# Shifting the six places of a weight ring by 16 bytes from one to the next

## What is computed

```python
x = x + 0.5 * swiglu(rmsnorm(x, ffn1_norm[l]), w_ffn1_in[l], w_ffn1_out[l])
u = rmsnorm(x, mix_norm[l])
c_q, c_kv, k_r, hq, hf, hi, hgate, mq, gate_logits = split_sizes(u @ w_in[l], IN_SPLITS)
y_mla, y_hg, y_mem = ... # three branches: latent attention, gated recurrence, memory attention
gates = jax.nn.sigmoid(gate_logits.reshape(B, S, N_BRANCH, D))
merged = gates[:, :, 0] * y_mla + gates[:, :, 1] * y_hg + gates[:, :, 2] * y_mem
x = x + merged @ w_out[l]
x = x + 0.5 * swiglu(rmsnorm(x, ffn2_norm[l]), w_ffn2_in[l], w_ffn2_out[l])
```

## The kernel before, in words

| operand | start past a multiple of 128, before | after |
|---|---|---|
| places 0 to 5 of `upper` | 96 each | 96, 112, 0, 16, 32, 48 |
| places 0 to 5 of `ring` and `rest` | 96 each | 32, 48, 64, 80, 96, 112 |
| `xT_upper`, `xT_rest` | 0 | 0 |
| `hT`, `OT`, `memory`, `Sc`, `PT` | 96 | 96 |
| `x`, `xn` | 96 | 64 |
| `G`, `O`, `par`, `cst`, `sil` | 0 | 0 |
| `arena` | 64 | 64 |

## Time and profile before

### The profile page before, as it was taken

The page is one execution under the profiler, slowest core; times in us unless marked ns, Lnnn a source line. Parts: engine busy times, 40 slices in busy tenths (PEclk is TensorE's granted clock), DMA queues, the critical chain, the costliest instruction groups (busy, mean ns, idle before and its releaser), DMA issues.

```text
span 2621.8 us, 48248 instructions
## 1 busy us (share of the span) xinstructions
PE 2583.0 (99%) x19726; PEld 2371.5 (90%) x19726; DVE 868.4 (33%) x1518; ACT 1285.9 (49%) x1934; POOL 2032.4 (78%) x906
## 2 busy tenths in 40 slices
PE   7999999999999999999999999999999999999998
PEld 6999999899899989989989998998998989899897
DVE  2644364211232436411121133733122131473212
ACT  4445555444444555544444444745444444574443
POOL 7988666798898856788888886468888878547886
PEclk9999999999999999999999999999999999999999
DMA  6566543555656654666655556245556556525664
GB/s 235 186 202 200 185 137 130 194 191 188 211 183 198 204 181 137 166 195 187 190 197 187 184 188 214 91 161 193 192 179 205 191 177 194 193 98 174 196 190 139
DMA packets 128738, 474.79 MB, mean 181 GB/s; under 512 B 14432, under 2 KB 14432, under 8 KB 127520
## 3 DMA queue, kind: packets, MB, share of 16 engines
q1 hardware_dynamic: 124704, 454.09, 53.1%
q0 software_dynamic: 3840, 17.83, 2.4%
HBM read 469.24 MB, written 2.62 MB: 180 GB/s over the span
## 4 chain that ended last, share of the span: by engine, by line
PE 91%; DVE 5%; ACT 2%; DMA 1%; issue 1%; POOL 1%; DVEq 0%; SPq 0%; ACTq 0%; POOLq 0%
PE psA L381 51%; PE psY L381 38%; PE psT L432 2%; DMA ring<-in_weights 1%; DVE psY L1279 0%; POOL rest L1065 0%; ACT upper L1876 0%; DVE psY L1267 0%; PE psT L654 0%; DMA cst<-in_consts 0%; DVE st L1364 0%; DVE x L1294 0%; ACT xT_upper L1876 0%; ACT G L1907 0%; DVE Sc L1339 0%
## 5 line engine op out<-in xcount | busy, mean ns | idle before, releaser
L1065 POOL TENSOR_TENSOR rest<-ring,upper 128x1024 fp32r<-128x1024 f32 (+1 forms) x834 | 1992.8, 2409 | 524.5 <-ACT upper L1876 513.9
L1876 ACT ACTIVATE upper<-ring 128x1024 fp32r<-128x1024 f32 (+1 forms) x834 | 870.2, 1053 | 787.4 <-DMA ring<-in_weights 786.9
L381 PE MATMUL psA<-xT_upper,upper 128*128 128x256 f32 x2784 | 383.1, 280 | 0.6 <-ACT arena L1876 0.6
L381 PE MATMUL psA<-xT_upper,rest 128*128 128x256 f32 x2784 | 381.1, 279 | 0.0
L381 PE MATMUL psA<-xT_rest,upper 128*128 128x256 f32 x2784 | 381.1, 279 | 0.0
L1320 DVE TENSOR_TENSOR psA<-sil,psA 128x256 f32<-128x256 f32 x144 | 61.8, 429 | 936.4 <-ACT sil L1876 936.3
L381 PEld LDWEIGHTS psA<-xT_upper,upper 128*128 128x128 f32 x2784 | 359.3, 188 | 12.8 <-ACT arena L1876 1.3
L381 PEld LDWEIGHTS psA<-xT_rest,upper 128*128 128x128 f32 x2784 | 349.4, 188 | 0.0
L381 PEld LDWEIGHTS psA<-xT_upper,rest 128*128 128x128 f32 x2784 | 349.4, 188 | 0.0
L381 PE MATMUL psY<-upper,hT_upper 128*128 128x512 f32 x704 | 202.6, 393 | 1.9 <-DVE hT_rest L1322 1.9
L381 PE MATMUL psY<-upper,hT_rest 128*128 128x512 f32 x704 | 200.4, 390 | 0.0
(11 more groups left out here) (282 smaller groups left out, 3003.7 us busy)
## 6 DMA issues: line engine op xcount, KB each, us to landing
ring<-in_weights SPq DMA_DIRECT2D x862, 512.0 KB, 3.8
G<-in_rows POOLq DMA_DIRECT2D x6, 1024.0 KB, 7.5
G<-in_rows POOLq DMA_DIRECT2D x7, 512.0 KB, 6.6
arena<-rel_by_distance POOLq DMA_DIRECT2D x8, 256.0 KB, 7.4
x<-in_x SPq DMA_DIRECT2D x2, 512.0 KB, 6.1
par<-in_params POOLq DMA_DIRECT2D x4, 256.0 KB, 5.6
xn<-in_mem POOLq DMA_DIRECT2D x1, 1024.0 KB, 11.1
memory_transposed<-arena POOLq DMA_DIRECT2D x1, 1024.0 KB, 5.5
```

The lines of the kernel that those rows point to most:

```text
L381: i = pe.matmul(out, lhsT, rhs, start=start, stop=stop)
L1065: pool.tensor_tensor(rest[:, r, 0:n], ring[:, r, 0:n], upper[:, r, 0:n], ALU.subtract)\
L1876: act.activation(out, in_, func, **kw).then_inc(*up)
```

## The change

The places of `upper` and of `ring` (with `rest`) become 1028 numbers wide, of which the first 1024 are used; each place starts 4112 bytes behind the one before it, where it was 4096. `before_turned` grows from 8 to 16 numbers, and constants are taken off `slots` and `steps`, so that the starts in the table above result. `xT`, `hT`, `OT` and `memory` keep theirs modulo 128. The instructions of every engine, their shapes and their order are the same ones as before.

```diff
--- before.py
+++ after.py
@@ -35,6 +35,7 @@
 LOW = -1.0e29
 
 PIECE = 1024
+PAD = 4
 R = 6
 PIECES = (218, 213)
 LAYERS = 2 * DEPTH
@@ -154,22 +155,22 @@
 
 
         sb("before_upper", [P, 24])
-        upper = sb("upper", [P, R, PIECE], F32R)
+        upper = sb("upper", [P, R, PIECE + PAD], F32R)[:, :, 0:PIECE]
         x = sb("x", [P, TT, D])
         xn = sb("xn", [P, TT, D])
-        sb("before_turned", [P, 8])
+        sb("before_turned", [P, 16])
         xT = (sb("xT_upper", [P, KD, S], F32R), sb("xT_rest", [P, KD, S], F32R))
         G = sb("G", [P, 24, S])
         O = sb("O", [P, TT, 512])
         overlay = SB_END - 4 * 6 * 4 * S
-        slots = overlay - 4 * R * PIECE
-        steps = slots - 4 * 16 * S
+        slots = overlay - 96 - 4 * R * (PIECE + PAD)
+        steps = slots - 64 - 4 * 16 * S
         Sc = nc.alloc_sbuf_tensor_at("Sc", [P, 2, 4, S], F32, offset=steps)
         PT = nc.alloc_sbuf_tensor_at("PT", [P, 2, 2, 4, P], F32, offset=steps + 4 * 8 * S)
         hT = tuple(nc.alloc_sbuf_tensor_at(n, [P, HIDDEN, S], F32R, offset=steps + 4 * i * HIDDEN * S)
                    for i, n in enumerate(("hT_upper", "hT_rest")))
-        ring = nc.alloc_sbuf_tensor_at("ring", [P, R, PIECE], F32, offset=slots)
-        rest = nc.alloc_sbuf_tensor_at("rest", [P, R, PIECE], F32R, offset=slots)
+        ring = nc.alloc_sbuf_tensor_at("ring", [P, R, PIECE + PAD], F32, offset=slots)[:, :, 0:PIECE]
+        rest = nc.alloc_sbuf_tensor_at("rest", [P, R, PIECE + PAD], F32R, offset=slots)[:, :, 0:PIECE]
         OT = nc.alloc_sbuf_tensor_at("OT", [P, 6, 4, S], F32, offset=overlay)
         turned_parts = (nc.alloc_sbuf_tensor_at("OT_upper", [P, 3, 4, S], F32R, offset=overlay),
                         nc.alloc_sbuf_tensor_at("OT_rest", [P, 3, 4, S], F32R, offset=overlay + 4 * 3 * 4 * S))
```

## The result

The changed kernel takes **2646.4 us** (median of four runs, 2645.5 to 2647.4); beside it on the same chip the kernel before takes 2621.8 us (2619.8 to 2624.6). The ratio is 1.0093, interval 1.0078 to 1.0107: slower by 24.6 us, where +11.3 had been forecast. The measured time lies inside the range.

What follows compares the result with a forecast made beforehand. The prediction took TensorE's instruction spacings as the bound, set by its two operands' start distance modulo 128. Its terms, +16.1 - 2.1 + 2.8 - 5.5 = +11.3 us, gave 2632 us, with an overall range of 2580 to 2656.

Steps and rivals of the forecast that it cites:

- the period of six: Sign in TensorE's timeline: xT passes of 8 would vary from piece to piece, repeating every six ring places, mean near 0.945 us.
- rival "nothing": TensorE's spacings differ for reasons other than distance, so the ring's start is neutral: 2620 us, chance 0.16.
- rival "GpSimd as the bound": GpSimd's subtraction slows on oddly aligned rows and makes TensorE wait in the feed-forward stages: 2684 us, chance 0.04.
- the faster rival: TensorE's operand streams collide less at distances other than 0 and 32, so spacings fall: 2592 us, chance 0.38.
- unseen distances: Operand distances without a profile row, given the middle of two known spacings: 118.3 ns for 256 columns, 230.0 for 512.
- Step 1: Matmuls moving xT over upper or rest, 256 columns, 10,800 in all: slower by 16.1 us.
- Step 2: Matmuls moving OT and memory over the ring, 256 columns, 1344 in all: faster by 2.1 us.
- Step 3: Matmuls moving the ring over stationary hT, 512 columns, 2112 in all: slower by 2.8 us.
- Step 4: Matmuls moving the ring over stationary xT, mostly 512 columns, 1728 in all: faster by 5.5 us.
- Steps 5 to 8: x and xn starts, GpSimd's subtraction, ScalarE's copy and the weight transfers: each claimed to change nothing.
- The low bound: Best spacing allowed for unseen 256-column distances, 113.3 ns; with the other classes' low ends it gave 2577 us.
- The high bound: Worst spacing allowed for unseen 256-column distances, 120 ns; with the other classes' high ends it gave 2657 us.

Runs made afterwards that it cites:

- m1: Separate kernel, TensorE alone reading one tensor at stepped operand distances, then at both kernels' addresses; before's places 2.80 us each, the changed kernel's 2.84 to 2.88 us.
- e1: Kernel before with xT and everything allocated behind it 128 bytes further on, nothing else changed: 2638.8 us, ratio 1.0064.
- e2: Kernel before with only upper's places 4112 bytes apart, ring, rest and hT as before, xT where the changed kernel has it: 2645.5 us, ratio 1.0090.
- m2: Separate TensorE-only kernel: distances in 4-byte steps, and rounds of six xT and three hT passes; 48 xT matmuls at distance 192 took 5.82 or 5.61 us.
- b2: Kernel before, pitch 4096 kept, with xT, hT, OT and memory all moved to 192 bytes past the weights' places: 2597.7 us, ratio 0.9917.

## Why the prediction was right, and where not

**The direction and the place were right.** The loss is in TensorE's spacings alone, it goes with the distance of TensorE's own two operands, and the period of six showed. The rival "nothing" falls with every class of the table; the rival "GpSimd as the bound" with 2401 ns in the mean and 1.5 us of waits for rest; the faster rival with spacings that rose in all xT classes. m1 shows the two kernels' spacings with the other engines at rest. The direction was held with little confidence, 0.43 against 0.37 for faster, and hung on two values out of sixteen.

**The size was under half, +11.3 against +24.6.** Two steps failed, and they are not the same.

*The mechanism: "distance" was taken modulo 128, with one spacing to a distance.* The prediction named its own test, whether the spacings at 0 and 32 keep 120.0 and 116.5, and they do not: place 0 of upper, at 32 modulo 128, has 119.1 ns, e1 moves nothing modulo 128 and costs 17.0 us, and e2 shows a class that changes with its distance kept. In the sum itself this weighs little. Of the prediction's own counts, the 1280 with upper at place 0 would have been unseen (+2.1 us) and the 896 taken for distance 0 too (-1.5 us), and the forecast would have moved by under 1 us.

*The size: the values given to unseen distances, 230.0 ns for 512 columns above all.* By terms, with the matmuls matched one by one:

- Step 1, xT moving, had +16.1 and measured +20.3 us. Rest stationary was right (+4.8, measured +4.9). Upper stationary had +11.3 and measured +15.4: the 1280 that "keep distance 32 and cost nothing" were at 160 and paid 1.8 us, and the rest of it is that the places of upper met no good distance. The middle value of 118.3 ns is close to the mean of both 256-column rows of m1 (118.2), which is luck, for two values.
- Step 2, OT and memory, had -2.1 and measured -2.4. Right.
- Step 3, hT stationary, had +2.8 and measured +8.2. Distance 0 is, with 240, the best value for 512 columns (226.8 to 227.8); the mean of that row is 231.9, and the three kinds came to 232.5, 231.0 and 233.2, above the 230.0 taken.
- Step 4, xT stationary, had -5.5 and measured -1.0: the passes fell by at most 0.8 ns. The places at 128 modulo 256 were taken for distance 0 and given 226.7 ns, a value of the hT class; for the others the 230.0 was as low as in step 3.
- Steps 5 to 8, all at nothing, held: all other matmuls, transposes among them, +0.5 us; 3.8 us of waits for the ring against 3.9; GpSimd 2401 ns; landing 3.4 us. The 96 matmuls with memory stationary were left out of the sum, and took +0.3.

Of the 14.1 us between +11.3 and the +25.4 of the matched matmuls, steps 3 and 4 hold 9.9 and step 1 holds 4.2. The low bound, 113.3 ns, was one step under the better of two values, and nothing in the rows pointed to it. That the sweep has just this value at 112 and 192 is luck. The high bound of 120 was too low: place 1 of upper has 120.4, and the sweep reaches 123.4.

What the prediction said of the Trainium skill, page "SBUF — State Buffer", section "Who interferes with whom" (TensorE never waits on anyone), agrees with m1 so far as others go: at before's addresses 116.7 ns with every other engine idle, and 116.6 to 117.0 in the whole kernel. The N/2.4 + 2.5 ns of the Trainium skill, page "TensorE: Matmul & The Clock Gate", section "Back-to-back issue gap", by which 256 columns would take an estimated 109.2 ns, was reached by no class in these runs; the best spacing of a pass is 113.2.

**What stays open.** Why a distance has its value, why the stationary start modulo 32 changes it, and what picks between the two states of distance 192 was not found; the sweeps show only that addresses and what ran before do it, with every other engine idle. Whether some layout holds the kernel in the state of 113.4 ns throughout was not tried, and neither was distance 112 in the whole kernel, though all of its rounds in m2 settled there.

## What to carry to other kernels

When TensorE is 99% busy and the spacings of equal matmuls differ by class, list the start address of each operand modulo 256, not modulo the alignment that the code happens to keep, and measure each pair in a small kernel of TensorE alone before moving anything. One such kernel of 578 us gave the sign and roughly the size of the change (+16 to +32 us by the pass taken, +24.6 measured). Where two known values must stand for many unseen ones, do not take their middle for the mean: for 512 columns it was 2 to 3 ns low, and that was more than half of the miss. A layout in which all places have one good distance beats a scatter, which brings the mean (here +22.5 us with xT in its old place). And check a table's best entry inside the real sequence of passes, since a distance can have two states and a pass depends on those ahead of it: the table promised -52 us and gave -10, and the sweep with whole rounds led to -23.5.

## What was unexpected of the hardware

- With no other engine at work, 256-column matmuls have spacings from 113.3 to 123.4 ns at 16-byte steps, by (moving start - stationary start) modulo 256 bytes and by the stationary start modulo 32 (m1_sweep, second passes); 512-column ones 226.8 to 235.0. That is 9% and 4% at equal shapes, clock and order.
- The same instructions at the same addresses run at 117.8 or 113.4 ns, with every other engine idle, and stay so for a round of 48 (m2_fine).
- A pass depends on the passes ahead of it: at distance 0, 512 columns take 226.5 or 231.2 ns by the distance of those ahead (m2_fine), and in e2 a class whose two operands did not move rose from 226.8 to 232.5 ns.
- A 128-byte shift of one buffer is worth 0.64% of the whole kernel (e1), a better layout -0.83% (b2), without one instruction changed.
